# Mix layers: the first half of the merged rows turned on VectorE between the gate products

## What is computed

```
g = sigmoid(gates).reshape(bsz, S, 3, 1024)
merged = (g[:, :, 0] * (y_a @ w_branch_a) + g[:, :, 1] * (y_b @ w_branch_b)
          + g[:, :, 2] * (y_c @ w_branch_c))
x = x + merged @ w_out
x = x + 0.5 * swiglu_ffn(x, ffn2_norm, ffn2_w_gate, ffn2_w_up, ffn2_w_down)
```

## Time and profile before

| | us |
|---|---|
| median of 3 runs | 1827.95 (1827.79 to 1828.08) |
| the profiled execution, its own time | 1828.98 |
| its span in the trace | 1827.2 |
| PE busy | 1806.8 (99%) |
| POOL busy | 1364.8 (75%) |
| DVE busy | 916.0 (50%) |
| ACT busy | 911.6 (50%) |

### The profile page before, as it was taken

One profiled execution on the slowest core, in us unless ns is written; L12 is line 12 of the kernel. 1 busy time (PEld: TensorE's weight loads), 2 busy tenths in 40 slices (PEclk: granted clock), 3 DMA queues, 4 the chain that ended last, 5 costly groups with the idle time before them and its releaser, 6 DMA issues.

```text
span 1827.2 us, 25144 instructions
## 1 busy us (share of the span) xinstructions
PE 1806.8 (99%) x9394; PEld 1491.3 (82%) x9394; DVE 916.0 (50%) x1690; ACT 911.6 (50%) x1351; POOL 1364.8 (75%) x568
## 2 busy tenths in 40 slices
PE   6999999999999999999999999999999999999999
PEld 5888788887889888887788888888888878888887
DVE  4673766778654524855553230713195565143152
ACT  3324524674456644456554644464445555545452
POOL 2624544559968898977689798969897868898885
PEclk9999999999999999999999999999999999999999
DMA  9852785739675675565465566557655645656653
GB/s 367 293 201 70 265 308 165 197 122 315 228 266 199 207 215 194 183 196 160 135 185 195 175 194 194 196 185 233 192 192 184 187 130 163 193 163 210 192 194 127
DMA packets 194841, 363.96 MB, mean 199 GB/s; under 512 B 32261, under 2 KB 48373, under 8 KB 194165
## 3 DMA queue, kind: packets, MB, share of 16 engines
q1 hardware_dynamic: 191856, 354.87, 60.9%
q10 hardware_dynamic: 2884, 7.73, 1.1%
HBM read 361.50 MB, written 6.10 MB: 201 GB/s over the span
## 4 chain that ended last, share of the span: by engine, by line
PE 98%; DMA 0%; DVE 0%; ACT 0%; ACTq 0%; issue 0%; POOL 0%
PE ps L1233 26%; PE ps L1235 26%; PE ps L1234 26%; PE ps L1359 3%; PE ps L1360 3%; PE ps L1361 3%; PE ps L1939 1%; PE ps L1940 1%; PE ps L1941 1%; PE ps L1281 1%; PE ps L1491 1%; PE ps L1866 1%; PE ps L1645 1%; PE ps L1616 1%; PE ps L1626 1%; PE ps L1911 1%
## 5 line engine op out<-in xcount | busy, mean ns | idle before, releaser
L587 POOL TENSOR_TENSOR w_lo<-raw,w_hi 128x1024 fp32r<-128x1024 f32 x556 | 1345.9, 2455 | 413.5 <-ACT w_hi L625 392.4
L1233 PE MATMUL ps<-w_hi,act_rows_r 128*128 128x512 f32 x2064 | 817.0, 396 | 3.8 <-POOL w_lo L587 3.1
L1235 PE MATMUL ps<-w_hi,act_rows_r 128*128 128x512 f32 x2064 | 806.0, 390 | 0.0
L1234 PE MATMUL ps<-w_lo,act_rows_r 128*128 128x512 f32 x2064 | 805.4, 390 | 0.0
L625 ACT ACTIVATE w_hi<-raw 128x1024 fp32r<-128x1024 f32 x556 | 571.4, 1058 | 357.1 <-DMA raw<-in_ffn_w_up 99.3
L1233 PEld LDWEIGHTS ps<-w_hi,act_rows_r 128*128 128x128 f32 x2064 | 388.5, 188 | 90.9 <-issue 8.8
L1235 PEld LDWEIGHTS ps<-w_hi,act_rows_r 128*128 128x128 f32 x2064 | 388.2, 188 | 81.8
L1234 PEld LDWEIGHTS ps<-w_lo,act_rows_r 128*128 128x128 f32 x2064 | 388.8, 188 | 76.8
L2584 DVE STREAM_TRANSPOSE ps<-proj 32x256 f32<-32x256 f32 (+1 forms) x384 | 166.6, 434 | 6.5
L2565 DVE TENSOR_TENSOR proj<-proj,ps 128x1024 f32<-128x1024 f32 (+1 forms) x18 | 20.4, 1133 | 252.2 <-PE ps L1235 247.8
L1359 PE MATMUL ps<-act_rows_r,w_hi 128*128 128x512 f32 (+1 forms) x288 | 101.4, 352 | 0.0
(11 more groups left out here) (243 smaller groups left out, 1557.2 us busy)
## 6 DMA issues: line engine op xcount, KB each, us to landing
raw<-in_w_in SPq DMA_DIRECT2D x120, 512.0 KB, 3.7
raw<-in_ffn_w_gate SPq DMA_DIRECT2D x88, 512.0 KB, 4.4
raw<-in_ffn_w_up SPq DMA_DIRECT2D x88, 512.0 KB, 4.4
raw<-in_ffn_w_down SPq DMA_DIRECT2D x88, 512.0 KB, 4.2
proj<-in_ada_w SPq DMA_DIRECT2D x39, 512.0 KB, 8.3
pt<-in_ada_w SPq DMA_DIRECT2D x38, 512.0 KB, 6.5
raw<-in_pool_w_in SPq DMA_DIRECT2D x32, 512.0 KB, 7.8
raw<-in_na_w_in SPq DMA_DIRECT2D x32, 512.0 KB, 5.7
```

The source lines that it names most:

```text
L587: pool.tensor_tensor(w_lo[:, s, :], raw[:, s, :], w_hi[:, s, :].bitcast(F32), ALU.subtract).then_inc(lo_done, 1)
L1233: pe.matmul(o, h, hi, start=start, stop=False)
L1234: pe.matmul(o, h, lo, start=False, stop=False)
L1235: return pe.matmul(o, c, hi, start=False, stop=stop)
```

## The change

Half 0 of `merged` is turned by DVE instead of PE. DVE's 16 transposes (line 2079 in the changed kernel) come in two runs of eight: the first behind the addition of j = 2, the second behind the gate product of j = 3, ahead of the two low parts. ACT's high parts of k = 0 and 1 now wait for the second run. PE loses `turn_merged(0)` and `turn_merged(1)`, and at the start of `mix_out` it waits for both low parts of half 0 where it waited for the first, and for the banks. Half 1 is turned by PE as before. This happens in both mix layers.

```diff
--- before.py
+++ after.py
@@ -1124,7 +1124,10 @@
                             y_high(br)
                 split(9)
                 for k in range(4):
-                    act.wait_ge(pe_done, pe_s.count(("tp", f"m{l}", 0, k)))
+                    if k < 2:
+                        act.wait_ge(dve_done, dve_s.count(("tp", f"m{l}")))
+                    else:
+                        act.wait_ge(pe_done, pe_s.count(("tp", f"m{l}", 0, k)))
                     act.wait_ge(group_used, end_of(stage) + 1)
                     act.activation(xt_hi[0][:, 2 * k:2 * k + 2, :], ps[:, MERGED_BANK[k], :].rearrange("p (c n) -> p c n", c=2),
                                    ACT.Copy).then_inc(act_done, act_s.one(("xhi", f"m{l}", 0, k)))
@@ -1960,18 +1963,13 @@
                         pe.wait_ge(acc_free[(bb + j) % 2], reads(bb + j - 2))
                     for k in range(2):
                         branch_group(j, k)
-                        if j == 4 and k == 0:
-                            for n in (13, 14):
-                                pe.wait_ge(acc_free[(b + n) % 2], reads(b + n))
-                            turn_merged(0)
-                            turn_merged(1)
 
                 go, bo = G0[f"mix_out{l}"], B0[f"mix_out{l}"]
-                read_out(0)
-                read_out(1)
+                for k in range(2):
+                    pe.wait_ge(dve_done, dve_s.count(("xt", f"m{l}", 0, k)))
                 for k in range(4):
                     s = weights(go + k)
-                    if k % 2 == 0:
+                    if k == 0:
                         pe.wait_ge(dve_done, dve_s.count(("xt", f"m{l}", 0, k // 2)))
                     for t in range(NT):
                         for nb in range(2):
@@ -2888,6 +2886,14 @@
                                       xt_hi[0][:, 2 * k:2 * k + 2, :].bitcast(F32), ALU.subtract)\
                        .then_inc(dve_done, dve_s.one(("xt", f"m{l}", 0, k)))
 
+                def merged_turned(some):
+
+                    dve.wait_ge(dve_done, dve_s.count(("merged", l, 0)))
+                    for n in (13, 14):
+                        dve.wait_ge(acc_free[(b + n) % 2], reads(b + n))
+                    return squares_turned(lambda q, n: free(ps[32 * q:32 * q + 32, MERGED_BANK[0], 0:1], [[SEQ, 4], [P, NT], [1, 32]], n),
+                                          lambda i, n: free(proj[32 * i:32 * i + 32, 0:1], [[P, 4], [IN_COLS, NT], [1, 32]], GATES + n), some)
+
                 for j in range(6):
                     nb, br = j // 3, j % 3
                     dve.wait_ge(group_used, gb + 2 * j + 2)
@@ -2898,7 +2904,10 @@
                         dve.wait_ge(acc_free[(bb + j) % 2], reads(bb + j))
                         m = pj(GATES + nb * 512, 512, IN_COLS)
                         dve.tensor_tensor(m, m, v, ALU.add).then_inc(dve_done, dve_s.one(("merged", l, nb) if br == 2 else ("msum", l, nb)))
+                    if j == 2:
+                        merged_turned((0, 1))
                     if j == 3:
+                        merged_turned((2, 3)).then_inc(dve_done, dve_s.one(("tp", f"m{l}")))
                         merged_low(0)
                         merged_low(1)
                 merged_low(2)
```

## The result

| | before | after |
|---|---|---|
| median of 11 runs, us | 1828.16 (1827.79 to 1834.08) | 1836.25 (1834.09 to 1837.83) |
| ratio after to before, 95% interval | | 1.0041 (1.0033 to 1.0049) |
| span of the profiled execution, us | 1827.2 | 1834.5 |

The change makes the kernel slower by 0.41%, 7.5 us by the ratio. The forecast was 1834.3 in a range of 1830 to 1838. Two further runs of the kernel before, beside the first four experiments, took 6447 and 10395 us and are left out of every comparison.

The account below looks back on a forecast made before the run. PE was taken as the bound, busy 1806.8 of 1827.2 us. Two layers losing 3.2 us each, saving included, add 6.3 to the profiled 1828.98, giving 1835.3; the median lies 1.03 lower, so 1834.3, range 1830 to 1838.

Parts of the forecast that it names:

- The saving on PE: Before the output projection, PE without its eight transposes saves 0.87 us per mix layer, 1.74 us in two.
- DVE's transposes: Eight take 3.76 us on DVE, in two runs around the gate product of j = 3; POOL is not slowed.
- The delay of ACT's pair: ACT's pair of high parts of half 0 begins at 1003.8 instead of 999.21, 4.6 us later.
- POOL's late start: POOL, waiting for ACT's first weight split behind the pair, goes on at 1005.9 instead of 1001.32.
- POOL's stretch: Weight pieces at 2.37 us, additions costing 1.0 each; w_out 7 ready at 1024.5, PE beginning it 3.2 us later.
- The two waits: In the output projection's first tile PE waits 1.4 us for w_out 6 and 1.6 us more for w_out 7.
- The wait for half 1: PE waits 0.7 us for DVE's addition of j = 5, swallowed by the later wait for w_out 7.
- The rival of POOL keeping up: At w_out 6 and 7 POOL is in time, so not slower: 1826.2 to 1827.6; chance 12%.
- the additions are free: DVE's additions cost POOL nothing in their new places, w_out 7 ready 2.0 us earlier per layer: 1830.2; chance 7%.
- The clock: Rival: PE's clock falls in the new waits, giving 1837.7 for one fall, 1841.1 for one per layer; chance 8%.
- a single fall: PE's clock falls once in the new waits, giving 1837.7; half of the 8% given to falls.
- The sum without the term: Loss over two mix layers without a clock fall: 2 x 3.2 = 6.3 us, PE's saving already counted.

Follow-up runs that it names:

- the first four experiments: Changed kernel with one, two or four weight splits ahead of ACT's pair; kernel before with ACT's pair held. Ratios 1.0008, 0.9996, 1.0004, 1.0065.
- all sums from PSUM, two splits ahead: Changed kernel with all four additions reading the gate product from PSUM, w_out 1 and 2 split before ACT's pair: 1827.07 us, ratio 0.9993.
- the longer hold: Kernel before, ACT's pair of high parts of half 0 held until PE finishes the first piece of j = 5: 1840.62 us, ratio 1.0065.
- the shorter hold: Kernel before, ACT's pair held only until PE finishes the second piece of j = 4: 1832.13 us, ratio 1.0025.
- the sums of half 1 from PSUM: Changed kernel with the additions of j = 4 and 5 reading the gate product from PSUM: 1830.74 us, ratio 1.0014.

## Why the prediction was right, and where it was not

- **The saving on PE**, 0.87 us per layer: in the changed kernel PE enters the output projection at 1006.13 + 0.60 = 1006.73, 0.91 us earlier than before. In the version in which it waits for nothing new (all sums from PSUM, two splits ahead), 0.89 per layer is left at the next stage. Right.
- **DVE's transposes**: eight in 3.74 us (3.76 forecast), POOL not slowed by them (its four pieces beside the first run take 11.48 us, 11.42 before). Right.
- **The delay of ACT's pair**, 4.6 us: 4.60 measured.
- **POOL's late start**, 1005.9: 1005.92. The cause was put to the test from both sides. Moving two splits out from behind the waiting pair removes the loss with DVE's work unchanged, and holding the pair with PE's work unchanged makes it.
- **POOL's stretch**, seven pieces and two additions of 1.0 us: w_out 7 forecast to begin at 1024.6, measured 1024.44. The two waits, forecast at 1.4 and 1.6 us from start to start, are 1.5 each in the same terms (1.35 in the view); the cost per layer, forecast at 3.2, is 3.11 in the stage.
- **The wait for half 1**, 0.7 forecast: 0.6 from start to start (0.5 in the view), and swallowed as said.
- **The rival of POOL keeping up** fell with that; "the additions are free" fell too: freed in an experiment, they gave back the 1.0 us each of the sum.
- **The clock** is where the forecast was short. The median of 1836.25 lies just outside the 1832 to 1836 that I had given 70%. It is inside the stated range only because that range took in a single fall, to which I had given 4%: that is luck, since the reasoning called a fall unlikely. I had put 8% on a fall, because the new waits were shorter than the one at the start and had matmuls between them. The step that failed is this comparison with the one wait of 3.09 us: the clock fell at the second of two waits of 1.35 us, one microsecond apart, in one layer of two.
- **What the fall cost.** The profiled run has a fall in its second mix layer, (1 - 0.72) x 6 / 0.5 = 3.4 us at the lower level, which cost 1.65 us. Ten of its eleven runs show a mean clock of 0.997 or 0.998; of the 25 runs of the kernel before beside the first four experiments 17 show 0.999, 7 show 0.998 and one 1.000. I had taken the fall's length from the start's 6.8 us; it was half of that here, and as long as that in one layer of the longer hold. The sum without the term, 6.3, is what the undisturbed runs show: 1834.09 less 1827.48 is 6.6, one run of each. With one fall it is 8.0, near the difference of the medians, 8.1, or 7.5 by the ratio. That most runs have just one such fall is not shown: only one execution was traced, and mean clocks of 0.997 and 0.998 do not tell where the clock fell.

The Trainium skill's caution (TensorE: Matmul & The Clock Gate, § Why this matters for your kernels) is about idle gaps between bursts of matmuls that are longer than these. The windows above show a fall with gaps of only 1.35 us, so here the measurement goes further than the page. For the additions, SBUF — State Buffer, § Who interferes with whom, says that a VectorE instruction with two SBUF inputs contends with a GpSimd instruction that reads SBUF, that the lock is exclusive, and that an instruction with at most one SBUF input, outside the two-port modes, does not contend. The trace agrees on both. Beside a working POOL the additions with both inputs in SBUF take from 1.22 us, where one meets the end of a piece, to 3.24, and those with one input in SBUF 1.22 each time.

## What to carry to other kernels

Before work is moved off the bounding engine, follow the queue behind every instruction whose release gets later: here a wait grew on ACT, which idled anyway, and the five weight splits behind it starved POOL, whose margin towards PE was 0.9 us and stood in no view of waits. What stands behind the wait can be put ahead of it, but only as far as it does not collide anew; here two splits were better than four. And where VectorE has to add beside a busy GpSimd, one operand left in PSUM spares both of them the exclusion.

## What the runs showed of the hardware that I had not expected

The granted clock fell to its lower level (1.2 of 2.4 GHz) at waits of 1.35 us. In the profiled runs it fell in one layer of two where two such waits came about one microsecond apart behind one of 0.5 us (the changed kernel), in both layers where that first one was 1.0 us (the longer hold), and in neither layer where a single wait of 1.36 us came (the shorter hold) or one of 1.35 us with a delay of 0.3 us ahead (the sums of half 1 from PSUM). A fall of 3.4 us cost 1.65 us. These are one execution of each kernel, with two layers each, and what decides stays open.

The fall at the kernel's start differs between executions of the same work, too. The window from 20 to 30 us of the changed kernel's profile has 0.83, where the kernel before had 0.66:

```profile
20.00:30.00 10.00, 6.91 (x41) 5.23 (x45) 7.00 (x22) 5.15 (x11) 4.73 (x2) 0.83 1.04 388
```

That is 3.4 us at the lower level instead of 6.8. The work behind it comes 1.1 us earlier (PE's eight transposes at 32.47 before begin at 31.41), not the 1.7 us that half speed alone would give. The kernel before agrees: its runs with a mean clock of 0.999 and of 0.998, which falls of 3.4 and 6.8 us would give, have medians 1.1, 1.4 and 1.4 us apart in the three comparisons. No edit here touches this. In a study of tenths of a per cent the runs are better compared at the same mean clock.
